# Cross attention of a hybrid mLSTM block: scores as three fp32r products, and one place for the queries

## What is computed

```
X_HEADS = 4;  X_DH = 256
def cross_attn(xn, memn, w_q, w_kv, w_o):
    q = (xn @ w_q).reshape(Bsz, S, X_HEADS, X_DH)
    k, v = jnp.split(memn @ w_kv, 2, axis=-1)
    ...
    s = jnp.einsum('bshd,bmhd->bhsm', q, k).astype(F32) * (X_DH ** -0.5)
    p = jax.nn.softmax(s, axis=-1).astype(v.dtype)
    o = jnp.einsum('bhsm,bmhd->bshd', p, v).reshape(Bsz, S, D)
    return o @ w_o
h = h + cross_attn(rmsnorm(h, norm_x[i]), memn, x_w_q[i], x_w_kv[i], x_w_o[i])
```

## Time and profile before

| | us |
|---|---|
| median of 3 runs | 1418.3 (1417.88 to 1418.78) |
| the profiled execution, its time | 1416.5 |
| the profiled execution, its span | 1414.5 |
| PE busy | 1374.5 |
| DVE busy | 946.9 |
| ACT busy | 493.8 |
| POOL busy | 203.3 |

### The profile page before, as it was taken

How to read it: one execution, slowest core, us unless ns; L and a number is a source line. 1 busy time by engine, 2 the same in 40 slices (tenths; PEclk the granted TensorE clock), 3 DMA queues, 4 the chain that set the end, 5 groups by cost and what they waited for, 6 DMA issues and landing times.

```text
span 1414.5 us, 18133 instructions
## 1 busy us (share of the span) xinstructions
PE 1374.5 (97%) x6833; PEld 1163.5 (82%) x6833; DVE 946.9 (67%) x1660; ACT 493.8 (35%) x868; POOL 203.3 (14%) x228
## 2 busy tenths in 40 slices
PE   7999999999998989999999999999999998999997
PEld 6988889889887878888877888888888886788887
DVE  5838458458476873454577976677787778877765
ACT  6323313213334453231334533343444433222222
POOL 4101201202213000000005000000000003444441
PEclk9999999999999999999999999999999999999999
DMA  5111211201312221010133132244444448889702
GB/s 180 38 53 31 60 31 31 60 30 31 105 60 90 90 65 55 30 60 0 60 112 112 45 113 93 79 164 157 142 141 164 150 170 331 279 307 318 238 30 120
DMA packets 108822, 156.43 MB, mean 111 GB/s; under 512 B 6400, under 2 KB 67904, under 8 KB 108352
## 3 DMA queue, kind: packets, MB, share of 16 engines
q1 hardware_dynamic: 108736, 155.28, 32.6%
HBM read 112.79 MB, written 42.47 MB: 110 GB/s over the span
## 4 chain that ended last, share of the span: by engine, by line
PE 88%; DVE 6%; issue 3%; ACT 1%; SPq 1%; POOL 1%; DMA 1%; POOLq 0%; ACTq 0%; DVEq 0%
PE PS L1851 14%; PE PS L1853 13%; PE PS L1852 13%; PE PS L2170 8%; PE PS L2168 8%; PE PS L2169 8%; PE PS L2198 4%; PE PS L2200 4%; PE PS L2199 4%; PE PS L2054 2%; PE PS L1993 1%; DVE SG L1412 1%; PE PS L1914 1%; PE PS L1995 1%; PE PS L1997 1%
## 5 line engine op out<-in xcount | busy, mean ns | idle before, releaser
L1851 PE MATMUL PS<-XH,WH 128*128 128x512 f32 (+1 forms) x448 | 175.1, 391 | 4.7 <-issue 4.7
L1852 PE MATMUL PS<-XL,WH 128*128 128x512 f32 (+1 forms) x448 | 168.4, 376 | 0.0
L1853 PE MATMUL PS<-XH,WL 128*128 128x512 f32 (+1 forms) x448 | 168.4, 376 | 0.0
L1496 DVE TENSOR_TENSOR xT<-PS,xT 128x512 f32<-128x512 f32 x128 | 87.7, 690 | 46.2 <-PE PS L1853 45.7
L1702 DVE TENSOR_TENSOR xT<-PS,xT 128x512 f32<-128x512 f32 x120 | 81.1, 689 | 44.9 <-PE PS L2200 44.5
L1851 PE MATMUL PS<-YH,WH 128*128 128x512 f32 x256 | 101.5, 396 | 0.7 <-issue 0.7
L1851 PEld LDWEIGHTS PS<-XH,WH 128*128 128x128 f32 x448 | 84.7, 189 | 20.9 <-issue 5.8
L1853 PE MATMUL PS<-YH,WL 128*128 128x512 f32 x256 | 99.8, 390 | 0.0
L1852 PE MATMUL PS<-YL,WH 128*128 128x512 f32 x256 | 99.7, 389 | 0.0
L1853 PEld LDWEIGHTS PS<-XH,WL 128*128 128x128 f32 x448 | 84.8, 189 | 15.8
L1852 PEld LDWEIGHTS PS<-XL,WH 128*128 128x128 f32 x448 | 84.8, 189 | 14.5
(11 more groups left out here) (386 smaller groups left out, 3465.5 us busy)
## 6 DMA issues: line engine op xcount, KB each, us to landing
forms_hi<-HS SPq DMA_DIRECT2D x56, 256.0 KB, 2.4
raw<-in_f_w_up_dram SPq DMA_DIRECT2D x11, 1024.0 KB, 6.0
rawE<-in_f_w_gate_dram SPq DMA_DIRECT2D x10, 1024.0 KB, 6.1
raw<-in_f_w_down_dram SPq DMA_DIRECT2D x40, 256.0 KB, 3.9
raw<-in_a_w_in_dram SPq DMA_DIRECT2D x8, 1024.0 KB, 5.4
forms_lo<-U SPq DMA_DIRECT2D x32, 256.0 KB, 2.6
XH<-forms_hi SPq DMA_DIRECT2D x16, 512.0 KB, 6.7
XL<-forms_lo SPq DMA_DIRECT2D x12, 512.0 KB, 7.6
```

Source lines behind the costliest of these rows:

```text
L1496: v.tensor_tensor(xt, PS[:, g % NB, :], xt, ALU.add).then_inc(s_fd, 1)
L1851: mm(dst, wh, xh, start=(k == 0), stop=False)
L1852: mm(dst, wh, xl, start=False, stop=False)
L1853: last = mm(dst, wl, xh, start=False, stop=(k == len(tiles) - 1))
```

## The change

Keys and queries get a high and a low part in fp32r, and the scores become three matmuls for each 128 features, by the same `product` as everywhere else. So a quarter has 12 score matmuls in place of 4 calls. The keys are split in two pieces (6 and 2 of the 8 tiles of 256 columns) by new parts `ksplit`, in front of groups 1 and 2 of query strip 0; the split of the values moves one group later each. A query group is no longer copied out by ACT alone: ACT writes the high part QHH, then DVE subtracts it from the bank and writes the low part QHL, and the bank is counted free in `s_fd` by DVE. QHH and QHL have one place each, for all heads. Therefore ACT's copy of group 0 of head h waits for the scores of quarters 0 and 1 of head h - 1, and that of group 2 for quarters 2 and 3.

```diff
-    BY_ACT = {"v", "o", "mk", "mv", "q", "gate"}
+    BY_ACT = {"v", "o", "mk", "mv", "gate"}
...
     for t in range(2):
-        part("q", 0, 1 + t, ("vsplit", t, None))
+        part("q", 0, 1 + t, ("ksplit", t, None))
+        part("q", 0, 2 + t, ("vsplit", t, None))
...
-        QH = [VQ[:, 1].rearrange("p (a s) -> p a s", a=2), SG[:, :, :]]
+        KMH = [sb_at("KMH", [P, 6, M], late_at + 8192, F32R), sb_at("KMT", [P, 2, M], scan_at + 8192, F32R)]
+        KML = sb_at("KML", [P, 2 * H, M], qk_at, F32R)
+        QHH = sb_at("QHH", [P, 2, S], vv_at + 8192, F32R)
+        QHL = sb_at("QHL", [P, 2, S], place["SG"], F32R)
...
# ACT
+            def ksplit(t, b):
+                act.wait_ge(s_fa, FREED[FIRST[AT["mk", H - 1]]][1])
+                act.wait_ge(s_yl, H * TT)
+                sc.activation(KMH[t][:, :, :], KM[:, 6 * t:6 + 2 * t, :], ACT.Copy).then_inc(s_kvh, 1)
...
+                if kind == "q":
+                    act.wait_ge(s_mm, g + 1)
+                    if r == 0 and h == 0:
+                        act.wait_ge(s_b, TT * H)
+                    if r % 2 == 0 and h >= 1:
+                        act.wait_ge(s_sc, 4 * (h - 1) + 2 + r)
+                    sc.activation(QHH[:, r % 2, (r // 2) * HALF:(r // 2 + 1) * HALF], bank, ACT.Copy).then_inc(s_qh, 1)
+                    return
...
-                elif kind == "q":
-                    if r == 0 and h == 0:
-                        act.wait_ge(s_b, TT * H)
-                    if r == 0 and h == 1:
-                        act.wait_ge(s_xl, LO[3, LATE[1]][1])
-                    if r == 0 and h >= 2:
-                        act.wait_ge(s_sc, 4 * (h - 1))
-                    sc.activation(QH[h % 2][:, r % 2, (r // 2) * HALF:(r // 2 + 1) * HALF], bank,
-                                  ACT.Copy).then_inc(s_fa, 1)
...
# DVE
+            def ksplit(t, b):
+                dve.wait_ge(s_kvh, 2 * t + 1)
+                at = slice(6 * t, 6 + 2 * t)
+                v.tensor_tensor(KML[:, at, :], KM[:, at, :], KMH[t][:, :, :].bitcast(F32), ALU.subtract).then_inc(s_kvl, 1)
...
+                elif kind == "q":
+                    hi, lo = (t[:, r % 2, (r // 2) * HALF:(r // 2 + 1) * HALF] for t in (QHH, QHL))
+                    dve.wait_ge(s_qh, 4 * h + r + 1)
+                    v.tensor_tensor(lo, PS[:, g % NB, :], hi.bitcast(F32), ALU.subtract).then_inc(s_fd, 1)
...
# PE
-                        pe.wait_ge(s_fa, FREED[FIRST[AT["q", h]] + 3][1])
+                        pe.wait_ge(s_fd, FREED[FIRST[AT["q", h]] + 3][1])
+                        pe.wait_ge(s_kvl, 3)
...
-                        for kk in range(2):
-                            last = mm(PS[:, NB + e % 2, j * M:(j + 1) * M], QH[h % 2][:, kk, at], KM[:, 2 * h + kk, :],
-                                      start=(kk == 0), stop=(kk == 1))
+                        keys = lambda k: (KMH[k // 6][:, k % 6, :], KML[:, k, :])
+                        last = product(PS[:, NB + e % 2, j * M:(j + 1) * M],
+                                       [((QHH[:, kk, at], QHL[:, kk, at]), keys(2 * h + kk)) for kk in range(2)])
...
-                            pe.wait_ge(s_vml, MT)
+                            pe.wait_ge(s_kvl, 2 * MT)
```

More of the change, by code:

```diff
@@ L430, in build_block @@
         s_pah = sem("s_pah")
-        s_vmh = sem("s_vmh")
-        s_vml = sem("s_vml")
+        s_kvh = sem("s_kvh")
+        s_kvl = sem("s_kvl")
+        s_qh = sem("s_qh")
         s_pv = sem("s_pv")
@@ L803, in _ @@
             todo = {"scan": scan, "memnorm": memnorm, "sumsq": sumsq, "pieces": pieces}
-            for what in ("gates", "memturn", "spread", "attn", "vsplit"):
+            for what in ("gates", "memturn", "spread", "attn", "vsplit", "ksplit"):
                 todo[what] = lambda a, b: None
@@ L998, in vsplit @@
                 act.wait_ge(s_fa, FREED[FIRST[AT["mv", H - 1]]][1])
-                sc.activation(VMH[:, t, :], VM[:, t, :], ACT.Copy).then_inc(s_vmh, 1)
+                sc.activation(VMH[:, t, :], VM[:, t, :], ACT.Copy).then_inc(s_kvh, 1)
+            def ksplit(t, b):
+                act.wait_ge(s_fa, FREED[FIRST[AT["mk", H - 1]]][1])
+                act.wait_ge(s_yl, H * TT)
+                sc.activation(KMH[t][:, :, :], KM[:, 6 * t:6 + 2 * t, :], ACT.Copy).then_inc(s_kvh, 1)
             todo = {"gates": gates, "scan": scan, "memnorm": memnorm, "memturn": memturn,
-                    "pieces": pieces, "attn": attn, "vsplit": vsplit}
+                    "pieces": pieces, "attn": attn, "vsplit": vsplit, "ksplit": ksplit}
             for what in ("sumsq", "spread"):
@@ L1484, in vsplit @@
             def vsplit(t, b):
-                dve.wait_ge(s_vmh, t + 1)
-                v.tensor_tensor(VML[:, t, :], VM[:, t, :], VMH[:, t, :].bitcast(F32), ALU.subtract).then_inc(s_vml, 1)
-            todo = {"gates": gates, "scan": scan, "memnorm": memnorm, "memturn": memturn, "vsplit": vsplit,
+                dve.wait_ge(s_kvh, 2 * t + 2)
+                v.tensor_tensor(VML[:, t, :], VM[:, t, :], VMH[:, t, :].bitcast(F32), ALU.subtract).then_inc(s_kvl, 1)
+            def ksplit(t, b):
+                dve.wait_ge(s_kvh, 2 * t + 1)
+                at = slice(6 * t, 6 + 2 * t)
+                v.tensor_tensor(KML[:, at, :], KM[:, at, :], KMH[t][:, :, :].bitcast(F32), ALU.subtract).then_inc(s_kvl, 1)
+            todo = {"gates": gates, "scan": scan, "memnorm": memnorm, "memturn": memturn, "vsplit": vsplit, "ksplit": ksplit,
                     "sumsq": sumsq, "spread": lambda a, b: None, "pieces": pieces, "attn": attn}
@@ L2085, in _ @@
             todo = {"gates": gates, "scan": scan, "memnorm": lambda a, b: None, "memturn": memturn, "sumsq": sumsq,
-                    "spread": spread, "pieces": lambda a, b: None, "attn": attn, "vsplit": lambda a, b: None}
+                    "spread": spread, "pieces": lambda a, b: None, "attn": attn, "vsplit": lambda a, b: None, "ksplit": lambda a, b: None}
             def turn_x(t):
```

## The result

| | before | changed |
|---|---|---|
| median, us | 1418.54 (4 runs) | 1444.02 (1443.08 to 1445.37, 4 runs) |
| ratio | | 1.0184 (95%: 1.017 to 1.0198) |
| the profiled execution, its time | 1416.5 | 1444.28 |
| its span | 1414.5 | 1442.5 |

A forecast was written before the change was run, and what follows sets the result against it. PE (TensorE), 97% busy, was taken to bound the kernel. The terms -4.5 + 23.4 + 0.6 + 0.6 + 0.3 gave +20.4 us on the 1418.3 median: 1438.7 us, range 1430 to 1447 (8 in 10).

The forecast's parts named there:

- PE sets the time of the stage, so what it waits for counts in full: Cross attention, 540 to 720 us: PE busy 179.65 of 180 us, so any wait of PE shows in full.
- Scores 1.72 to 1.44, -4.5: Score sets: 12 matmuls at 0.120 us take 1.44 us in place of 1.72; 16 sets save 4.5 us.
- Twelve stalls, 23.4: Heads 1 to 3, behind query groups: transposes wait for DVE's scaling, 2.31 us at nine sites, 0.87 at three.
- The second wait of ACT's copy, 8.6 of the 23.4: Groups 0 and 2: ACT's query copy waits for the previous head's scores; without this cost, 8.6 us less.
- First scores +0.6: Behind the first head's last query group: scores also wait for DVE's low part, T+1.80 against T+1.17, +0.6 us.
- restarts +0.6: At the 12 stall sites: transposes to next matmul 0.41 us after a wait, 0.36 without, 0.6 us together.
- last head +0.3: Last output strips: one existing stall of 0.25 us grows because PE comes 0.28 earlier, +0.3 us.
- Key splits hidden: First query strip: key splits cost about 2.1 us on ACT and 2.5 on DVE, within 5 us of cover.
- The clock stays at 1.00: Attention stage: granted clock stays at 1.00 despite the stalls; the rival, a falling clock, +66 us, 1505, chance 0.02.
- the neighbouring rivals: Second wait costs little, 1430.1 us, chance 0.08; a DVE backlog at the 12 sites, 1447, chance 0.07.
- Nothing gives it back later: Stages after the attention: none recovers the loss, since PE bounds them too.
- one of the signs of being wrong: New profile: prediction wrong if the time before 534 us or behind 740 us changes by over a microsecond.

The follow-up runs named there:

- the run with the scaling first: The changed kernel, but DVE scales a quarter's probabilities ahead of the query group's low part instead of behind it; 1414.4 us, ratio 0.9975.
- the kernel with plain, longer scores: The kernel before plus one unused DVE subtraction behind 12 query groups and ACT's copy waiting for the previous head's scores; 1448.8 us, ratio 1.0214.
- the run with the filler: The changed kernel with unused matmuls on TensorE ahead of each of the 12 waits for DVE's scaling; 1438.0 us, ratio 1.0141.
- the sixth: The changed kernel with scaling first at all heads, plus unused matmuls before the first query strip and the first scores; 1410.1 us, ratio 0.9952.
- the two made from the kernel before: The kernel before plus an unused DVE subtraction behind 12 query groups, 1432.9 us; the same with ACT's copy waiting for the previous head's scores, 1448.8 us.

## Why the prediction was right

- *PE sets the time of the stage, so what it waits for counts in full.* Right: 158 us busy in place of 180 from 540 to 720, and the time grew by the stalls.
- *Scores 1.72 to 1.44, -4.5.* Right: 1.43 in the profile, and the run with the scaling first, in which they are nearly all that is left, is 3.9 us under the kernel before where my terms gave 3.6. The estimate by the count of passes of the Trainium skill (FP8 and Floating Point Precision, TensorE Precision Notes) was 1.29 a set; the trace, with 1.43, doesn't agree, and the row of a matmul of the same shape was the right price.
- *Twelve stalls, 23.4.* Right, each within 0.05 us; shown are 23.5 with the two old waits, 21.7 without, against "some 21". The row that made this possible was the earlier trace rows, an old wait of the same form.
- *The second wait of ACT's copy, 8.6 of the 23.4.* Right: 10.8 more of waits in the kernel with plain, longer scores.
- *First scores +0.6, restarts +0.6, last head +0.3.* The first is right (1.46 shown in place of 0.78, and the scores start at T+1.85 where T+1.80 was forecast). The restarts are right too: transposes to next matmul is 0.41 or 0.42 at all 12 sites. For the last head the reading was incomplete: behind its scores the transposes start at T+1.90, 2.05 and 1.90, where they started at T+1.95, 2.36 and 1.95 before. The first and third quarter, for which I had put nothing, thus lose 0.24 each of the 0.28 that the shorter scores give, and the second, for which I had put 0.3, loses nothing: about 0.6 with the restarts, in place of 0.3.
- *Key splits hidden.* Right: the two took 1.76 and 0.68 us on DVE and were done by 528.4, the first scores waited for the query's low part, and started at 533.90 us, no later than before (534.19).
- *The clock stays at 1.00.* Wrong. This is the step that failed: I had made the drop a rival with a chance of 0.02 and a price of 66 us, one whole group behind each stall. It came behind 5 of 12 sites at 1.7 us each, 6.8 net in the profiled execution, 6.0 by the run with the filler. Both the chance and the price were off, and the sum had no term for it: that the time still fell into the range is partly luck, since the range had been drawn from the bounds of the stalls and of the scores and from the neighbouring rivals, not from the clock. I had argued from one wait of 2.06 us in the trace of before, behind which the clock held. Five of the six experiments show a drop behind just this wait (the first has 0.53 from 512.5 to 515 us), and the sixth has it filled, so that one row was no evidence: whether the clock falls behind a wait of 2 us differs from site to site and from execution to execution. The rule of the Trainium skill (TensorE: Matmul & The Clock Gate, HAM oscillation) that a PE which idles between bursts goes back to the lower clock each time, pointed the right way; but the page's example waits longer between its bursts than PE does here, and here the clock fell behind five of nine waits of 2.1 to 2.2 us and behind none of 0.71.
- *Nothing gives it back later.* Right. But one of the signs of being wrong, a change of over a microsecond behind 740 us, was met in the profile (from the feed-forward's first matmul to the end 617.3 us before, 619.0 now), by the drop at 1210 us that the experiments show with either length. The sign was drawn too narrow for a single profiled execution.

## What to carry to other kernels

An instruction that is added to an engine with a fixed order costs what it makes the instructions behind it wait, not its own length: ask of each what it waits for, and who waits for what stands behind it. If such a wait can't be avoided, put everything that is ready ahead of it; here moving three short instructions turned +25.5 us into -4 and, with one more place, -9 (some 3 of these last 5 us are clock, which may be chance). And where TensorE is the bound, add to each sum of stalls of about 2 us a term for the clock behind them; here a quarter more. In the three kernels with such stalls unfilled (the changed one and the two made from the kernel before) a drop stands behind 11 of the 21 waits of 2.1 to 2.2 us and behind none of the 15 of 0.4 to 0.7.

## What the runs showed of the hardware that I had not expected

Unused matmuls in PE's waits made the kernel faster by 6.0 us (1444.0 to 1438.0) with the starts of the 12 waiting transposes, counted from their groups, unchanged to 0.01 us. A drop of the granted clock is not bound to one place: behind the same wait of 2.06 us at 511 us it is absent in the profile of before, of the changed kernel and of the run with that wait filled, and present in five others; behind the attention it comes and goes in the same way, at 1.7 us, and 3.4 in the last run (0.70, 0.50, 0.50 and 0.93 in four slices of 2.5 us). So a single profiled execution differs by a few us from another of the same kernel, and terms of this size need the median of several.
